# First fills with the norm's gain in the weights, products on the raw residual stream, the root applied to the tiles

## The reference, cut to what matters

```
layers = [(conv_attn_mixer, ..., mix0 gain, conv_ffn ..., ffn0 gain),
          (s5_mixer,        ..., mix1 gain, conv_ffn ..., ffn1 gain)]
for i in range(2):
    x = x + mixer(rms_norm_2(x, mix_g), ...)
    x = x + conv_ffn(rms_norm_2(x, ffn_g), ...)

rms_norm_2(x, g) = x * rsqrt(mean(x * x) + EPS) * g
conv_attn_mixer:  h = xn @ w_in; glu_a, glu_g, c_q, c_kv, k_r = split(h)
                  u = glu_a * sigmoid(glu_g); u = causal_dwconv(u, 31 taps) ...
conv_ffn:         h = causal_dwconv(xn @ w_up, 3 taps) + b
                  (silu(h[..., :2816]) * h[..., 2816:]) @ w_down
```

## Time and profile before

| what | value |
|---|---|
| median of 3 runs (lowest, highest) | 2749.92 us (2745.89, 2753.32) |
| the profiled execution's own time | 2748.43 us |
| its span | 2746.3 us |
| PE busy | 2671.5 us (97%), 12396 records |
| DVE, ACT, POOL busy | 1324.5, 624.3, 304.2 us |
| mean granted PE clock | 0.984 |

### The profile page before, as it was taken

The page is one execution under the profiler, slowest core; times in us unless marked ns, Lnnn a source line. Parts: engine busy times, 40 slices in busy tenths (PEclk is TensorE's granted clock), DMA queues, the critical chain, the costliest instruction groups (busy, mean ns, idle before and its releaser), DMA issues.

```text
span 2746.3 us, 31907 instructions
## 1 busy us (share of the span) xinstructions
PE 2671.5 (97%) x12396; PEld 1853.9 (68%) x12396; DVE 1324.5 (48%) x2846; ACT 624.3 (23%) x1152; POOL 304.2 (11%) x305
## 2 busy tenths in 40 slices
PE   8999999999999999999999998999999999999998
PEld 4777658898895655444444445588874484888887
DVE  2255556656642012000012775467766673777733
ACT  1155542312311112100011134221220022221201
POOL 0222134433432410000000000000000000000000
PEclk9999989999999998999999998999999999999999
DMA  4211111101013220344433210122223311222222
GB/s 188 77 47 62 47 46 47 47 32 47 35 43 109 97 77 29 140 173 174 164 107 107 75 48 16 69 92 78 92 93 107 107 49 55 84 92 81 88 92 92
DMA packets 32494, 226.98 MB, mean 83 GB/s; under 512 B 3552, under 2 KB 4192, under 8 KB 6112
## 3 DMA queue, kind: packets, MB, share of 16 engines
q1 hardware_dynamic: 30384, 219.50, 22.4%
q10 hardware_dynamic: 1968, 5.51, 0.6%
HBM read 222.90 MB, written 2.10 MB: 82 GB/s over the span
## 4 chain that ended last, share of the span: by engine, by line
PE 92%; DVE 5%; ACT 2%; issue 1%; POOL 0%; DMA 0%; DVEq 0%; ACTq 0%; POOLq 0%
PE psum L400 90%; DVE work L2703 1%; PE psum L897 1%; PE psum L1224 0%; DVE work L1800 0%; PE psum L2572 0%; PE psum L2246 0%; DVE hT L572 0%; PE psum L2058 0%; DVE work L1048 0%; DVE work L1794 0%; DMA mixT<-x_dram 0%; ACT work L611 0%; PE psum L634 0%; ACT work L975 0%
## 5 line engine op out<-in xcount | busy, mean ns | idle before, releaser
L400 PE MATMUL psum<-hT,ring 128*128 128x256 f32 (+3 forms) x2968 | 581.2, 376 | 10.9 <-ACT work L1349 6.1
L400 PEld LDWEIGHTS psum<-hT,ring 128*128 128x128 f32 (+2 forms) x2968 | 392.6, 163 | 166.6 <-issue 114.6
L400 PE MATMUL psum<-work,ring 128*128 128x512 f32 (+1 forms) x1208 | 418.5, 498 | 4.8 <-ACT work L3428 2.4
L400 PEld LDWEIGHTS psum<-work,ring 128*128 128x128 f32 x1208 | 228.3, 190 | 178.7 <-issue 156.4
L400 PE MATMUL psum<-work 128*128 128x128 f32 (+7 forms) x2390 | 327.0, 291 | 11.2 <-ACT work L2664 7.6
L400 PEld LDWEIGHTS psum<-work 128*128 128x128 f32 (+2 forms) x2390 | 275.7, 178 | 62.7 <-issue 32.1
L400 PE MATMUL psum<-work,mixT 128*128 128x256 f32 (+2 forms) x1332 | 290.9, 381 | 2.7 <-DVE work L2155 1.5
L400 PEld LDWEIGHTS psum<-work,mixT 128*128 128x128 f32 (+1 forms) x1332 | 232.7, 183 | 50.3 <-issue 16.9
L400 PE MATMUL psum<-ring,work 128*128 (+1 forms) x568 | 248.7, 596 | 2.2 <-issue 1.9
L400 PE MATMUL psum<-xT,ring 128*128 128x256 f32 x1024 | 242.5, 382 | 1.5 <-ACT mixT L752 1.3
L400 PEld LDWEIGHTS psum<-xT,ring 128*128 128x128 f32 x1024 | 188.2, 190 | 33.7 <-issue 6.4
(11 more groups left out here) (444 smaller groups left out, 2747.9 us busy)
## 6 DMA issues: line engine op xcount, KB each, us to landing
ring<-stream_dram SPq DMA_DIRECT2D x204, 1024.0 KB, 4.7
con<-consts_dram SPq DMA_DIRECT2D x1, 2953.0 KB, 13.3
mixT<-x_dram ACTq DMA_DIRECT2D x4, 512.0 KB, 6.5
work<-x_dram ACTq DMA_DIRECT2D x4, 512.0 KB, 6.2
out_dram<-mixT SPq DMA_DIRECT2D x4, 512.0 KB, 3.7
work<-p_dram ACTq DMA_DIRECT2D x1, 512.0 KB, 4.0
con<-ssm_dram ACTq DMA_DIRECT2D x1, 512.0 KB, 3.7
vec<-vecs_dram SPq DMA_DIRECT2D x1, 378.0 KB, 6.0
```

What stands on the lines that cost most here:

```text
L400: ins = self.eng.matmul(out, lhsT, rhs, start=start, stop=stop)
```

## The change

Four stages begin with a norm in the second block; three of them are changed: `mixer`, `ffn_a` and `ffn_b`. For each, POOL multiplies the stage's first fill in its ring slot by the norm's gain (`gained_fill_pool`, two operations of 128 x 1024), PE forms the first pair on `xT` in place of `hT` (`first_pair_pe`), with the norm's sums and root rows set between the chunk products of the first tile, and the root is multiplied onto the tiles' results. The unread products fall away in these three. The later fills still take `hT`, which DVE forms meanwhile. In `ffn_*` DVE multiplies the tile by the root (ACT copies the root to `rstd`) where ACT copied it, and the sums of the first seven-product fill move ahead of the stage mark (`first_sums_dve`). In `mixer` the first gate tile is copied by ACT, multiplied by the root on POOL, goes through the sigmoid on ACT, and is multiplied by the root again on POOL (for the value tile), before DVE's first `gated`. `ssm` opens as before.

```diff
@@ ple_pe, mixer_pe, ssm_pe: the call at their end is dropped @@
-            norm_sum_pe(e)
@@ mixer_pe @@
-            for j in range(3):
+            first_pair_pe(e, "mix0", chunk_told, 3)
+            e.c["h_ready"].n += DC
+            e.eng.wait_ge(S["h_ready"], e.c["h_ready"].at())
+            for j in range(1, 3):
                 w = slot()
-                tile_pe(blocks(w, 0, 8), h, h_ready if j == 0 else None)
+                tile_pe(blocks(w, 0, 8), h)
                 tile_pe(blocks(w, 8, 8), h)
@@ mixer_act @@
-            for j in range(3):
+            whole(gsig[:, 0, :])
+            e.skip(1)
+            e.eng.wait_ge(S["h_ready"], DC * (NORMS.index("mix0") + 1))
+            nc.scalar.activation(mix_root, root_bank, ACT.Copy).then_inc(S["root_out"], 1)
+            e.eng.wait_ge(S["gate_rooted"], 1)
+            nc.scalar.activation(gsig[:, 0, :], gsig[:, 0, :], ACT.Sigmoid).then_inc(S["gate_open"], 1)
+            for j in range(1, 3):
                 gate(j)
+        def first_gate_pool(e):
+            e.eng.wait_ge(S["root_out"], 1)
+            nc.gpsimd.tensor_tensor(gsig[:, 0, :], gsig[:, 0, :], mix_root, ALU.mult).then_inc(S["gate_rooted"], 1)
+            e.eng.wait_ge(S["gate_open"], 1)
+            nc.gpsimd.tensor_tensor(gsig[:, 0, :], gsig[:, 0, :], mix_root, ALU.mult).then_inc(S["gate_rooted"], 1)
@@ mixer_dve @@
+            e.eng.wait_ge(S["gate_rooted"], 2)
             gated(0)
@@ the first pair @@
-        def ffn_pe(e, before_last=None, closing=False):
-            e.eng.wait_ge(S[e.landing()], e.landed())
+        def first_pair_pe(e, gain, x_ready, sums_after=1):
+            fill_at[gain] = e.c["fill"].n
+            e.eng.wait_ge(S["gained_fill"], e.c["gained_fill"].next())
             w = e.slot(ring)
+            free = e.c["tile"].n
             for half in range(2):
-                e.eng.wait_ge(S["tile_free"], e.c["tile"].at(-1))
-                e.dense(e.bank(), blocks(w, 8 * half, 8), [hT[:, k, :] for k in range(DC)], h_ready if half == 0 else None)
+                e.eng.wait_ge(S["tile_free"], free + half - 1)
+                o = e.bank()
+                for k in range(DC):
+                    if half == 0:
+                        x_ready(e, free, k)
+                    ins = e.mm(o, blk(w, 8 * half + k), xT[:, k, :], k == 0, k == DC - 1)
+                    if half == 0 and k == sums_after:
+                        total_pe(e)
+                    if half == 0 and k == sums_after + 1:
+                        e.eng.wait_ge(S["col_root"], e.c["col_root"].next())
+                        root_rows_pe(e, root_bank, 0).then_inc(S["stage"], 1)
+                ins.then_inc(S["tile_done"], 1)
...
+        def ffn_pe(e, gain, x_ready, before_last=None, closing=False):
+            first_pair_pe(e, gain, x_ready, 3 if closing else 1)
...
+                if j == 0:
+                    e.c["h_ready"].n += DC
+                    e.eng.wait_ge(S["h_ready"], e.c["h_ready"].at())
                 product(0, a11, b11)
...
+                else:
+                    e.eng.wait_ge(S["root_out"], e.c["root_out"].next())
                 product(4, a12, b21)
+        def first_sums_dve(e):
+            for i in (0, 2, 1, 3):
+                weight_sum_dve(e, e.c["fast"].n, 0, i)
+        def gained_fill_pool(e, gain):
+            f = fill_at[gain]
+            e.eng.wait_ge(S["loaded%d" % (f % RING)], 16 * (f // RING + 1))
+            for half in range(2):
+                w = ring[:, f % RING, DC * P * half:DC * P * half + DC * P].rearrange("p (k n) -> p k n", k=DC)
+                ins = nc.gpsimd.tensor_tensor(w, w, bc(V(gain), P), ALU.mult)
+            ins.then_inc(S["gained_fill"], 1)
@@ ffn_act @@
-            for half in range(2):
-                e.eng.wait_ge(S["tile_done"], e.c["tile"].next())
-                nc.scalar.activation(fpad[:, half, 2:2 + T], e.result(), ACT.Copy).then_inc(S["tile_free"], 1)
-                e.eng.wait_ge(S["tile_free"], e.c["tile"].at())
+            e.eng.wait_ge(S["h_ready"], DC * (NORMS.index(gain) + 1))
+            nc.scalar.activation(rstd, root_bank, ACT.Copy).then_inc(S["root_out"], 1)
@@ ffn_dve @@
+            def rooted(half):
+                e.eng.wait_ge(S["tile_done"], e.c["tile"].next())
+                nc.vector.tensor_tensor(fpad[:, half, 2:2 + T], e.result(), rstd, ALU.mult).then_inc(S["tile_free"], 1)
...
+                if i == 3:
+                    e.eng.wait_ge(S["root_out"], e.c["root_out"].next())
+                    rooted(0)
                 nc.vector.tensor_tensor(h_sums[:, o, :, :], in0, in1, ALU.subtract).then_inc(S["h_sum"], 1)
+            rooted(1)
@@ the engines' programs @@
+            gained_fill_pool(e, "mix0")
+            first_gate_pool(e)
+            gained_fill_pool(e, "ffn0")
+            gained_fill_pool(e, "ffn1")
```

More of the change, by code:

```diff
@@ L2438, in program @@
         upad, ys, gsig = a(4, 30 + T), a(4, T), a(2, T)
+        mix_root = squares[:, DC - 1, :]
         m_s, m_pr, m_pt = a(2, T), a(2, T), a(2, T)
@@ L2734, in mixer_dve @@
             cos, sin = C("rope_cos"), C("rope_sin")
+            e.c["root_out"].next()
+            e.eng.wait_ge(S["gate_rooted"], 2)
             gated(0)
@@ L2956, in ffn_act @@
                 for half in range(2):
+                    if j == 0:
+                        e.eng.wait_ge(S["tile_free"], e.c["tile"].at(half - 1))
                     at = 6 * j + 3 * half + 2
@@ L3756, in _ @@
             ssm_pe(e)
-            e.eng.wait_ge(S["stage"], e.c["stage"].next())
+            e.c["stage"].next()
             e.mark("ffn_b")
-            ffn_pe(e, closing=True)
+            ffn_pe(e, "ffn1", chunk_mixed, closing=True)
         @block.scalar
```

66 lines of the change are left out of this document (38 added, 28 removed).

## The result

| what | before | changed kernel |
|---|---|---|
| median, lowest to highest | 2747.90 us (2744.53 to 2753.32, 4 runs) | 2727.99 us (2724.76 to 2729.89, 4 runs) |
| the profiled execution | 2748.43 us | 2724.76 us |
| its span | 2746.3 us | 2722.3 us |
| mean granted PE clock | 0.984 | 0.987 |

The ratio is 0.9923, with a 95% interval of 0.9903 to 0.9942: some 21 us faster. The forecast was 2726.9 us in a range of 2721 to 2733.5.

The account below looks back on a forecast made before the run. PE was taken as the bound (92% of the chain). Gain 30.68 - 7.53 - 0.10 = 23.05 us (mixer 8.90, `ffn_a` 2.98, `ffn_b` 11.17), so 2749.92 - 23.05 = 2726.9 us, range 2721 to 2733.5.

Parts of the forecast that it names:

- The gaps of 30.68 us go, 7.53 us of small work stays: PE, three openings: gaps of 11.41, 5.49 and 13.78 us removed; sums and root rows cost 2.51 us in each.
- The clock stays at 1.00: PE in mixer and `ffn_b` openings: granted clock 1.00 where it was 0.50, with real products where PE idled.
- The sums' waits: PE's first tile: no wait for squares in mixer or `ffn_a` (0.17 us to spare), 0.10 us in `ffn_b`.
- POOL's fill: Fill times gain on POOL: 5.4 us each, hidden; slower only from 27.6 us a fill, chance 0.02.
- POOL holds DVE: Rival: POOL's fills and gate hold DVE where PE waits; 18.8 us go back, 2745.6 us, chance 0.03.
- DVE follows in the feed-forward stages: First pass: third `h_sum` ready 0.7 us before product 1 in `ffn_b`, 2.4 in `ffn_a`; taps some 1.8 us later.
- DVE follows in the mixer: Mixer opening: gate ready at 1524.2, together with PE's second tile; `gated(0)` within 0.5 us behind it; 2.9 us slack.
- DVE late: Rival: DVE late in the openings, each losing 1 to 3 us; gain about 17 us, 2733 us, chance 0.12.
- The clock falls all the same: Rival: mixer and `ffn_b` openings still run at 0.50, losing 8.5 us; gain 14.5, 2735.4 us, chance 0.05.
- Nothing comes off: Rival: PE's gain is waited away behind DVE's taps in the mixer, and the rest likewise; 2749.9 us, chance 0.03.
- Nothing behind the openings moves: Behind the openings: no term in the sum; later feed-forward passes not longer than 12.1 us.

Follow-up runs that it names:

- no_unread: Kernel before without the three unread products in each of the three openings, nothing else changed: 2747.72 us, ratio 1.0001 to the kernel before.
- sums_first: Changed kernel with the norm's sums behind the tile's first product instead of the fourth, in mixer and `ffn_b`: 2733.28 us, ratio 0.9938 to the kernel before.
- fill_eight: Changed kernel with each half of the mixer's first fill multiplied by ones seven more times on POOL: 2746.19 us, ratio 0.9991 to the kernel before.
- sums_back: Changed kernel with the first fill's four weight sums back behind the `h_sum`s on DVE, both feed-forward stages: 2733.56 us, ratio 0.9940 to the kernel before.
- gate_late: Changed kernel with four more 128 x 512 POOL operations ahead of the mixer's gate: 2726.62 us, ratio 0.9918 to the kernel before.

## Why the prediction was right, point by point

- **The gaps of 30.68 us go, 7.53 us of small work stays.** Right. Three openings of 16.41 us where 13.74 + 2.51 = 16.25 was predicted: 0.16 us each too small, 0.5 in all. The two sets of sums take 1.70 us together and not 1.62, the product behind them 0.95 and not 0.86. One gap was misread, the 13.78 us of `ffn_b`: it was 13.48, so that 30.38 us go.
- **The clock stays at 1.00.** Right in every window of both openings. `no_unread` and `sums_first` show that it isn't a matter of course: it was lost behind waits of 0.66, 0.64 and 0.94 us in a row and behind one of 2.22, and kept behind one of 1.48. Real products as such aren't what keeps it: in `ffn_a` before, with unread ones and no wait, it was 1.00 as well.
- **The sums' waits.** The 0.10 us of `ffn_b` didn't come; it came of the same misreading: with 2316.76 for 2316.46 the sums stand at 2320.20, behind DVE's total at 2320.00. Openings together 22.4 us (predicted 23.05): less by 0.3 for the misread gap and by 0.5 for the openings' length, more by 0.1 for this wait. `sums_first` shows what the place of the sums is worth, 1.75 and 4.15 us.
- **POOL's fill.** Mis-sized: 3.75 us, not 5.4; the row of a 512-column operation without a broadcast was too dear a neighbour by the element (2.6 against 1.86 ns, 1351 / 512 and 1.90 us / 1024). Hidden either way, as `fill_eight` shows from the other end.
- **POOL holds DVE.** The mechanism, which the prediction said no run before showed alone, is there (0.69 to 2.27 us); its price for PE is nothing, as forecast, because DVE is not waited for in POOL's hours.
- **DVE follows in the feed-forward stages.** Right: the margin at product 1 is 1.05 us, predicted 0.7. The taps' delay against product 0 is 0.7 us (3.8 for 3.1), not 1.8. `sums_back` shows that the order of DVE's work holds this margin.
- **DVE follows in the mixer.** Right: `gated(0)` 0.3 us behind the tile, the gate ready at 1523.60 (16.57 us behind the last product of the stage before; predicted 1524.2, which is 16.54 behind it). `gate_late` shows the slack that was counted on, 4.4 us with the longer wait, not 2.9.
- **The other rivals.** DVE late: no wait for it in any of the openings. The clock falls all the same: not in the openings, but elsewhere, for a price of 1.7 us, below. Nothing comes off: no.
- **Nothing behind the openings moves.** Wrong by 1.7 us: the clock falls behind the latents' sums. The term was missing from the sum. By the traces the change is so worth 22.4 - 1.7 = 20.7 us, with which the ratios (21.2 and 19.2 us) agree; the forecast of 23.05 lies some 2 us too high, inside its own range. That the profiled pair shows 24.0 us comes of the attention's 2.5 us and the 0.6 us ahead of the mixer; both stretches vary as much among kernels with the same code there.
- **The forecast time was luck in part.** The changed kernel's median is 1.1 us from the forecast 2726.9 us. But the median of before was then 2747.90 us and not the 2749.92 that the forecast started from, and the medians differ by 19.9 us, not 23.05.

Why the clock falls behind the 24 sums of the changed mixer and not of the old one stays open: their own rows, and those for 60 us ahead of them, are the same in both within 0.1 us. The fall was there in 7 of 7 profiles of the changed opening as it is, and in none of the 5 others, and it goes when products stand between the sums. A high clock in the opening isn't the reason, for in `fill_eight` the opening ran at half the clock and the fall came all the same. The one changed mixer without it is `sums_first`, whose rows from the third tile to the sums are those of the changed kernel (61.80 us) and only stand 1.75 us later behind the stage before. So it looks as if it went by when the same work comes. If that is the cause, the 1.7 us are bad luck of this kernel's timing and no price of the idea; no run moved the sums alone, so it isn't shown.

## What to carry to other kernels

A norm ahead of a product needn't stand in the matrix engine's order: fold the gain into the weights on an idle engine, run the product on the raw stream, and put the root on the result; sums and root rows then cost their own length (2.7 us here) and no wait. Place the sums where the last total is already there, because a wait of 2.22 us cost 4.15 here, and give the waiting engine's predecessor (DVE's weight sums, here) its work in the order in which it is wanted. Before judging such an edit by single stretches, cut both traces at the same instructions: the attention behind it differed by up to 3.4 us from trace to trace, more than the 2.8 us of the smallest of the three parts.

## What the runs showed of the hardware that wasn't expected

- A multiplication with a broadcast operand on POOL, 128 x 1024, took 1.90 us, and 2.22 us where it started behind a held DVE operation (`fill_eight`). With 128 x 512 it took 1.04 to 1.11 us with a broadcast operand (`gate_late`) and 1.27 to 1.33 without: the broadcast one was the faster.
- A DVE operation with two SBUF inputs beside a row of POOL operations took 1.57 to 2.27 us for 0.69; with one SBUF and one PSUM input it took 0.69.
- The granted clock fell behind 24 one-column sums (2.73 us without a wait) and stayed when two chunk products stood among them; it fell behind a wait of 2.22 us and not behind one of 1.48 us. The same 24 sums behind the same 60 us of work had the fall in seven traces and not in five. These are single places, not a rule.
- Nine products that nobody reads, taken out, changed nothing that shows (1.0001, 0.9992 to 1.0010): their time came back as waits and half clock.
